# A two-layer decoder trunk on one core: the low halves of the weights are written over the raw weights, and a slot is loaded again only after TensorE has read it

## What is computed

```
h = h + 0.5 * rms(swiglu(rms(h, g0), ffn_w_in[0], ffn_w_out[0]), g1)
hn = rms(h, g2)
u_pool, q, k, v, gate_pool, gate_attn = split(hn @ w_in)
y_pool = pool_mixer(u_pool) @ w_pool_proj
y_attn = sliding_window_attention(q, k, v, sinks) @ w_attn_proj
h = h + rms((sigmoid(gate_pool)*y_pool + sigmoid(gate_attn)*y_attn) @ w_o, g3)
h = h + 0.5 * rms(swiglu(rms(h, g4), ffn_w_in[1], ffn_w_out[1]), g5)
```

## Time and profile before

| what | value |
|---|---|
| three runs | 1318.60, 1320.95, 1322.32 us; median 1320.95 us |
| profiled execution, first to last instruction (its span) | 1316.1 us |
| PE busy with products | 1273.8 us, 97% of the span |
| weight loads on PE (PEld) | 1225.1 us, 93% |
| DVE, ACT, POOL busy | 744.6, 530.2, 463.7 us |
| mean DMA rate | 150 GB/s |
| mean granted clock of PE | 0.987 |

### The profile page before, as it was taken

How to read it: one execution, slowest core, us unless ns; L and a number is a source line. 1 busy time by engine, 2 the same in 40 slices (tenths; PEclk the granted TensorE clock), 3 DMA queues, 4 the chain that set the end, 5 groups by cost and what they waited for, 6 DMA issues and landing times.

```text
span 1316.1 us, 26528 instructions
## 1 busy us (share of the span) xinstructions
PE 1273.8 (97%) x9877; PEld 1225.1 (93%) x9877; DVE 744.6 (57%) x1030; ACT 530.2 (40%) x738; POOL 463.7 (35%) x529
## 2 busy tenths in 40 slices
PE   6999999999999999999969999997999999999998
PEld 5999999998889999999969999997988899999997
DVE  5655444758556575544456554446586576655443
ACT  5333333435444443333424333334354444443331
POOL 2645501206322355541026545012063223655501
PEclk9999999999999999999989999998999999999999
DMA  8554456442255255535715544564522552654440
GB/s 268 192 170 160 130 167 203 140 157 65 65 128 193 97 192 168 175 123 161 231 40 194 190 141 131 176 191 138 160 65 65 128 193 97 219 184 159 145 156 32
DMA packets 203157, 197.11 MB, mean 150 GB/s; under 512 B 4168, under 2 KB 202032, under 8 KB 203072
## 3 DMA queue, kind: packets, MB, share of 16 engines
q1 hardware_dynamic: 202784, 195.69, 47.0%
q10 hardware_dynamic: 288, 0.27, 0.1%
HBM read 194.90 MB, written 1.05 MB: 149 GB/s over the span
## 4 chain that ended last, share of the span: by engine, by line
PE 81%; issue 10%; POOL 3%; DVE 3%; ACT 2%; DMA 0%; POOLq 0%; SPq 0%; DVEq 0%; ACTq 0%
PE bank L391 24%; PE bank L393 24%; PE bank L392 24%; PE bank L544 2%; POOL rt L1271 2%; PE bank L573 1%; ACT w_hi L688 1%; POOL acc L1267 1%; PE bank L473 1%; DVE tmp L947 1%; DVE x_lo L926 1%; PE bank L579 1%; DVE h L956 1%; POOL acc L1264 1%; PE bank L553 1%
## 5 line engine op out<-in xcount | busy, mean ns | idle before, releaser
L391 PE MATMUL bank<-x_hi,w_hi 128*128 128x272 f32 (+1 forms) x2048 | 599.2, 293 | 21.0 <-DVE x_lo L926 10.7
L393 PE MATMUL bank<-x_hi,w_lo 128*128 128x272 f32 (+1 forms) x2048 | 590.9, 289 | 0.0
L392 PE MATMUL bank<-x_lo,w_hi 128*128 128x272 f32 (+1 forms) x2048 | 589.2, 288 | 0.0
L875 DVE TENSOR_TENSOR w_lo<-raw,w_hi 128x2048 fp32r<-128x2048 f32 (+2 forms) x205 | 423.8, 2071 | 265.1 <-ACT w_hi L688 265.0
L688 ACT ACTIVATE w_hi<-raw 128x2048 fp32r<-128x2048 f32 (+2 forms) x216 | 357.1, 1658 | 519.8 <-PE bank L393 517.6
L391 PEld LDWEIGHTS bank<-x_hi,w_hi 128*128 128x128 f32 x2048 | 389.9, 190 | 30.9 <-issue 15.1
L392 PEld LDWEIGHTS bank<-x_lo,w_hi 128*128 128x128 f32 x2048 | 389.9, 190 | 0.3
L393 PEld LDWEIGHTS bank<-x_hi,w_lo 128*128 128x128 f32 x2048 | 389.7, 190 | 0.0
L391 PE MATMUL bank<-hid_hi,w_hi 128*128 128x272 f32 (+1 forms) x704 | 201.5, 286 | 0.0
L392 PE MATMUL bank<-hid_lo,w_hi 128*128 128x272 f32 (+1 forms) x704 | 201.3, 286 | 0.0
L393 PE MATMUL bank<-hid_hi,w_lo 128*128 128x272 f32 (+1 forms) x704 | 200.9, 285 | 0.0
(11 more groups left out here) (155 smaller groups left out, 1166.2 us busy)
## 6 DMA issues: line engine op xcount, KB each, us to landing
raw<-in_ffn_w_in SPq DMA_DIRECT2D x88, 1024.0 KB, 5.0
raw<-in_ffn_w_out SPq DMA_DIRECT2D x32, 768.0 KB, 4.4
raw<-in_w_in SPq DMA_DIRECT2D x24, 1024.0 KB, 5.5
raw<-in_ffn_w_out SPq DMA_DIRECT2D x32, 640.0 KB, 4.0
raw<-in_w_in SPq DMA_DIRECT2D x16, 512.0 KB, 4.8
raw<-in_w_attn_proj SPq DMA_DIRECT2D x32, 256.0 KB, 4.3
raw<-in_w_o SPq DMA_DIRECT2D x8, 1024.0 KB, 5.5
raw<-in_w_pool_proj SPq DMA_DIRECT2D x8, 512.0 KB, 3.3
```

The costliest lines, as they stand in the source:

```text
L391: pe.matmul(ps[:, t0:T], w[0], a_hi[:, t0:T], start=start, stop=False)
L392: pe.matmul(ps[:, t0:T], w[0], a_lo[:, t0:T], start=False, stop=False)
L393: return pe.matmul(ps[:, t0:T], w[1], a_hi[:, t0:T], start=False, stop=stop)
L875: last = dve.tensor_tensor(lo, w, hi.bitcast(F32), ALU.subtract)
```

## The change

The ring `w_lo` goes. Each slot's `w_lo` is now the same memory as its `raw`, seen as float32r, and DVE overwrites the raw weights with their low rest. So a load must wait until PE is done with unit `u-4` (`unit_done` in place of `lo_done`). The permutation of the query columns moves from the splits into the loads: four DMAs of 64 columns for each query unit in place of two of 128, and one split instruction on ACT and on DVE in place of two. Nothing uses the memory that becomes free.

```
 def unit_dmas(u):
-    return 2 if U_Q <= u < U_POOL else 4 if U_AP <= u < U_WO else 1
+    return 4 if U_Q <= u < U_POOL or U_AP <= u < U_WO else 1
...
-        raw = sb("raw", [P, RING, KD * UW])
+        raw = [sb(f"raw{s}", [P, KD * UW]) for s in range(RING)]
+        w_lo = [nc.alloc_sbuf_tensor_at(f"w_lo{s}", [P, KD * UW], F32R, offset=nc.sbuf_base - (RING - s) * KD * UW * 4)
+                for s in range(RING)]
         w_hi = sb("w_hi", [P, RING, KD * UW], F32R)
-        w_lo = sb("w_lo", [P, RING, KD * UW], F32R)
...
             s, n = u % RING, unit_k(u) * UW
-            if not U_Q <= u < U_POOL:
-                cuts = (0, n // 2, n) if halves else (0, n)
-                return [(raw[:, s, a:b], w_hi[:, s, a:b], w_lo[:, s, a:b]) for a, b in zip(cuts, cuts[1:])]
-            from_raw = raw[:, s, :].rearrange("p (k s t c) -> p t k s c", s=2, t=2, c=DH)
-            to_hi, to_lo = (w[:, s, :].rearrange("p (k t s c) -> p t k s c", s=2, t=2, c=DH) for w in (w_hi, w_lo))
-            return [(from_raw[:, t], to_hi[:, t], to_lo[:, t]) for t in range(2)]
+            cuts = (0, n // 2, n) if halves else (0, n)
+            return [(raw[s][:, a:b], w_hi[:, s, a:b], w_lo[s][:, a:b]) for a, b in zip(cuts, cuts[1:])]
...
             def slot_free(u, l, more=0):
 
-                sp.wait_ge(lo_done, l * UNITS + u + 1 + more)
+                sp.wait_ge(unit_done, l * UNITS + u + 1 + more)
...
                         c = q0 + (8 * ((u - U_Q) // 2) + 2 * ((u - U_Q) % 2)) * DH
-                        to = raw[:, u % RING, :].rearrange("p (k s c) -> p k s c", s=2, c=P)
-                        for side in range(2):
-                            load(u, w[:, :, c + side * 4 * DH:c + side * 4 * DH + P], to[:, :, side, :])
+                        to = raw[u % RING][:, :].rearrange("p (k t s c) -> p k t s c", s=2, t=2, c=DH)
+                        for t in range(2):
+                            for side in range(2):
+                                at = c + (side * 4 + t) * DH
+                                load(u, w[:, :, at:at + DH], to[:, :, t, side, :])
```

More of the change, by code:

```diff
@@ L300, in slot_free @@
             def slot_free(u, l, more=0):
-                sp.wait_ge(lo_done, l * UNITS + u + 1 + more)
+                sp.wait_ge(unit_done, l * UNITS + u + 1 + more)
             def load(u, src, dst=None):
                 s = u % RING
-                to = raw[:, s, 0:unit_k(u) * UW].rearrange("p (k c) -> p k c", c=UW) if dst is None else dst
+                to = raw[s][:, 0:unit_k(u) * UW].rearrange("p (k c) -> p k c", c=UW) if dst is None else dst
                 sp.dma_start(to, src).then_inc(raw_landed[s], 16)
@@ L356, in _ @@
                     slot_free(u, l)
-                    to = raw[:, u % RING, :].rearrange("p (g t c) -> p g t c", g=2, t=4)
+                    to = raw[u % RING][:, :].rearrange("p (g t c) -> p g t c", g=2, t=4)
                     for g in range(2):
@@ L386, in weights @@
                 s = u % RING
-                return [w[:, s, k * UW + mt * P:k * UW + (mt + 1) * P] for w in (w_hi, w_lo)]
+                c = slice(k * UW + mt * P, k * UW + (mt + 1) * P)
+                return [w_hi[:, s, c], w_lo[s][:, c]]
             def products(ps, w, a_hi, a_lo, start, stop, t0):
```

## The result

| what | before | after |
|---|---|---|
| median of the runs | 1320.9 us | 1419.7 us (1416.6 to 1426.5, 4 runs) |
| span of the profiled execution | 1316.1 us | 1417.4 us |
| PE busy | 1273.8 us | 1314.7 us |
| mean granted clock | 0.987 | 0.948 |

The ratio is 1.076, with a 95% interval from 1.073 to 1.079: 99 us slower. The forecast was 1400 us in a range from 1362 to 1440.

A forecast was written before the change was run, and what follows sets the result against it. PE was taken to bound the kernel (81% of the 1316.1 us span, DMA nothing). Waits of 65 us plus 14 us for the clock, on 1321 us, gave 1400 us; range 1362 to 1440 us.

The forecast's parts named there:

- steady first half: First feed-forward half: take of an up unit 9.8 us after a unit, PE wants its bank at 12.1; cost 0.
- starts of such a half: Start of a feed-forward first half: bank free at 9.8 us, wanted at 8.5; stall 1.3 us, three times, 4 us.
- ends of block 1 and of layer 0: Last squares wait behind ACT's split of a late unit: 5.8 us per block 1 end, 11.6 us; layer 0 end 3.5.
- around `w_o`: Both layers: squares and takes behind splits of units 66 to 68 end 5.5 us later; 11 us.
- K and V to the gates: Both layers: takes behind late query splits stall PE 3.2 and 3.4 us; gates start 7.1 us later; 14.2 us.
- behind the gates: Both layers: PE stalls 5.4 us at `attend(15)`, 1.5 before unit 60, then 3.3; together 20.4 us.
- the clock: Eight stops of 3 us or more amid PE's work, each followed by 3.41 us at half speed, costing 1.7: 14 us.
- rival 3: Query-unit loads: small pieces are dear, landing takes 9.8 us; 1415 us in all; chance 12%.
- Rival 1: Each of eight stops amid PE's work is followed by 10.24 us at clock 0.50; 1427 us; chance 15%.
- Rival 2: Feed-forward first halves: landing or in-place split 3.3 us longer holds PE 1 us at about 40 up units; 1440 us; 8%.
- Rival 4: Slack elsewhere absorbs the waits: half of 65 us and no clock term; 1355 us; chance 10%.
- Rival 5: All loads: landing wholly hidden if every take and square behind a split has over 5 us slack; 1321 us; 4%.

The follow-up runs named there:

- the last kernels: Changed kernel with lists moved at ends and middle, second half of low split waiting for rt: 1322.9 us; same lists, third ring and old wait: 1319.2 us.
- the two-ring kernel of 1322.9 us: Changed kernel with lists moved at ends and middle, low split halved ahead of boundary, second half waiting for POOL's rt: 1322.9 us, ratio 1.0015.

## Why the prediction was right, and where it was off

The direction, the mechanism and the places were right, and the time lay 20 us above the forecast. By its own steps:

| step | forecast, us | measured, us |
|---|---|---|
| steady first half | 0 | 0, as forecast |
| starts of such a half | 4 | 4.8 (`up_r`) |
| ends of block 1 and of layer 0 | 11.6 + 3.5 | 13.9 (`sq`) |
| around `w_o` | 11 | 11.7 (`acc`, 12.2 less the 0.5 of before) |
| K and V to the gates | 14.2 | 15.4 (`y` 7.2, `pool_u` 8.2) |
| behind the gates | 20.4 | 22.7 (`pT_meta` 11.3, `gates` 11.4) |
| sum of these | 65 | 68.5; 60.6 net of old waits that shrank |
| the clock | 14 | 41 (the rest of 101) |

- **What is removed, and in place.** Nothing, as forecast: the split in place takes 2.29 us, and the run with pieces and single splits alone is at 0.9995.
- **The landing of query units.** 7.3 us was taken from a line through two packet sizes; 7.2 was measured at unit 40, against 6.0 with pieces of 512 bytes. That it fits so well is partly luck: a packet took 21.9 ns and not the 19.5 of the line, and the four issues of SP, 2.1 us from first to last, are not in the forecast. The bound of 9.8 us (rival 3) did not come.
- **The waits.** Each was found by following one list past one late landing, and each group lies within 2.3 us of its forecast. That the net sum, 60.6, is below 65 comes from old waits, which the forecast left as they were. The two runs with moved lists confirm the reading: mend the order, and the wait goes while the landing stays late.
- **The clock is the step that was mis-sized**: "I take 1.7, since the shorter row is nearer in length". A stop of 5.65 us ahead of `attend(15)` was followed by 10.24 us at 0.50, with PE busy for 7.10 of them. By the rows at 0.50, the eight stops in the midst of PE's work had 38.6 us of busy time at half speed, so about 19 us in place of 14. The larger part of the error is in the next sentence, "PE is paced by DVE's `boundary` afterwards, so I add nothing there": behind the five stops at boundaries PE was busy 49.9 us at 0.50 (10.83 of 13.65 us, 9.50 of 10.24, and so on), up to 25 us more. The starts of halves and unit 60 were also left out, three stretches of 3.4 us. Together that is up to 49 us, of which 41 reached the end.
- **Rivals.** Rival 1 (long half-speed stretches, 1427 us) describes half of what happened: 10.24 us followed two of the eight stops, 6.8 one and 3.4 the other five. Rival 2 did not occur: the cover of 2.3 us in the steady halves held. Rival 4 (slack absorbs half) is visible in small: the old waits shrank by 7.9 us. In layer 1, PE's lag behind the kernel before shrinks by 2.1 us between the start of keys and values and the first query unit, where it waits for other things anyway. Rival 5 was wrong for this kernel, and its condition, more than 5 us of slack for every take and square, is what the last kernels build by hand.

Not tried: the freed memory as more slots. A deeper ring of raw weights should start loads earlier and take away the wait itself; no run shows it.

## What to carry to other kernels

When a load starts later, don't ask first whether its data still come in time. List what stands behind the instruction that consumes it, on that engine and on the next, and move ahead of it all that doesn't need it; ACT here then waited 581 us for landings, at a cost of 3.6 us. Check a moved or halved instruction against every count that its consumers wait for as a whole. And price a stop of TensorE at its own length plus half of the busy time that follows at the lower clock, at boundaries too.

## What was unexpected

- POOL's rt on 128x3 values takes as long as DVE lets it: 0.86 us at the shortest of its twelve times in the kernel before, 1.78 us beside a DVE split of 1.20 us, 2.85 us beside one of 2.27 us, so it ends 0.73 us after DVE does. In these cases the split had started 0.15 us ahead of rt. Where rt starts first, it takes 0.86 us beside the same half split, as here around `w_o` of layer 0 in the two-ring kernel of 1322.9 us:

```profile
453.09 0.86 POOL L1279 TENSOR_TENSOR rt<-var,half 128x3 f32<-128x3 f32 x1 [2.46 <-DVE var L916]
453.15 1.23 DVE L883 TENSOR_TENSOR w_lo<-raw,w_hi 128x1024 fp32r<-128x1024 f32 x1
```

  That agrees with the Trainium skill, page "SBUF — State Buffer", section "SBUF: two separate sides", by which a VectorE operation with two inputs in SBUF and a GpSimd operation that reads SBUF share a port pair, and whichever starts first has it for the whole instruction. It was worth 5.4 us here.
- A product of two 128x128 float32 identities took 0.227 us as two records at a granted clock of 1.00 (9.09 us for 40).
- In the midst of PE's work, stops of 3.0 to 3.8 us were followed by 3.4 us at 0.50, one of 4.55 us by 6.82, and ones of 5.1 to 6.2 us, there and at boundaries, by 10.24 or 13.65 us. Stops that look alike need not be followed by the same time: 3.44 us by 3.41, but 3.43 us at the end of layer 0 by 10.24.
